# Latent roots by a Newton step, and the rotary parts of two keys between the latents' pieces

## The reference

```python
def rms_norm(x, g):
    xf = x.astype(jnp.float32)
    y = xf * lax.rsqrt(jnp.mean(xf * xf, axis=-1, keepdims=True) + EPS)
    return (y * g.astype(jnp.float32)).astype(x.dtype)
...
def apply_rope(x, cos, sin):
    half = x.shape[-1] // 2
    x1, x2 = x[..., :half], x[..., half:]
    c = cos[None, :, None, :].astype(x.dtype)
    s = sin[None, :, None, :].astype(x.dtype)
    return jnp.concatenate([x1 * c - x2 * s, x2 * c + x1 * s], axis=-1)
...
    cq, ckv, kr, dq, dkk, dvv, nq, nkv, ng = jnp.split(h @ w_in, splits, axis=-1)

    qm = (rms_norm(cq, mla_q_norm_g) @ mla_w_uq).reshape(b, t, MLA_HEADS, MLA_NOPE_DIM + MLA_ROPE_DIM)
...
    kvm = (rms_norm(ckv, mla_kv_norm_g) @ mla_w_ukv).reshape(b, t, MLA_HEADS, MLA_NOPE_DIM + MLA_V_DIM)
...
    k_rope = apply_rope(kr[:, :, None, :], *cs_mla)[:, :, 0, :]
...
    k_all = apply_rope(kv[:, :, :, 0].reshape(b, t, 3 * NSA_GROUPS, NSA_DK), *cs_nsa).reshape(b, t, 3, NSA_GROUPS, NSA_DK)
    v_all = kv[:, :, :, 1]
    k_cmp = compress_tokens(k_all[:, :, 0], cmp_pos[0], cmp_w1[0], cmp_b1[0], cmp_w2[0])
```

## Time and profile before

| | us |
|---|---|
| three timed runs | 3837.71, 3849.64, 3850.16 |
| their median | 3849.64 |
| the profiled execution | 3834.81 |
| span of the profiled execution | 3832.8 |

### The profile page before, as it was taken

How to read it: one execution, slowest core, us unless ns; L and a number is a source line. 1 busy time by engine, 2 the same in 40 slices (tenths; PEclk the granted TensorE clock), 3 DMA queues, 4 the chain that set the end, 5 groups by cost and what they waited for, 6 DMA issues and landing times. The chain is left out here.

```text
span 3832.8 us, 50696 instructions
## 1 busy us (share of the span) xinstructions
PE 3603.5 (94%) x18374; PEld 2849.2 (74%) x18374; DVE 1356.9 (35%) x1911; ACT 1271.5 (33%) x1997; POOL 1410.6 (37%) x756
## 2 busy tenths in 40 slices
PE   7999799999999999799999996999998997779998
PEld 6888566688887888566688884888886784548886
DVE  4223554552325233554552326111115203561112
ACT  4222334443224222334443224312123234234222
POOL 4444333344444444333344442323232440014443
PEclk9999899999999999899999997999998998889999
DMA  4333343223323333343223332222212322013331
GB/s 133 97 99 88 73 125 107 93 77 99 95 88 99 98 98 89 72 127 106 94 77 99 94 89 70 60 66 60 66 52 58 88 77 66 1 44 88 94 98 60
DMA packets 569026, 322.34 MB, mean 84 GB/s; under 512 B 30266, under 2 KB 563360, under 8 KB 568480
## 3 DMA queue, kind: packets, MB, share of 16 engines
q1 hardware_dynamic: 568864, 320.22, 28.7%
HBM read 318.08 MB, written 2.10 MB: 84 GB/s over the span
## 5 line engine op out<-in xcount | busy, mean ns | idle before, releaser
L857 POOL TENSOR_TENSOR w_lo<-w_raw,w_hi 128x1024 fp32r<-128x1024 f32 x516 | 1268.4, 2459 | 2154.1 <-ACT w_hi L902 2154.1
L902 ACT ACTIVATE w_hi<-w_raw 128x1024 fp32r<-128x1024 f32 x516 | 546.9, 1061 | 1846.1 <-PE psum L2086 1731.6
L2086 PE MATMUL psum<-h_hi,w_hi 128*128 128x512 f32 x1296 | 529.7, 409 | 42.8 <-DVE h_ctx_lo L1482 21.8
L2086 PE MATMUL psum<-xg_hi,w_hi 128*128 128x512 f32 x1408 | 551.7, 392 | 13.7 <-DVE xg_lo L1434 12.1
L2086 PE MATMUL psum<-xg_lo,w_hi 128*128 128x512 f32 x1408 | 549.0, 390 | 0.0
L2086 PE MATMUL psum<-xg_hi,w_lo 128*128 128x512 f32 x1408 | 548.9, 390 | 0.0
L2086 PE MATMUL psum<-h_lo,w_hi 128*128 128x512 f32 x1296 | 513.0, 396 | 0.0
L2086 PE MATMUL psum<-h_hi,w_lo 128*128 128x512 f32 x1296 | 512.9, 396 | 0.0
L2086 PE MATMUL psum<-a_hi,w_hi 128*128 128x512 f32 x1232 | 432.8, 374 | 5.0 <-DVE a_lo L1550 4.2
L2086 PE MATMUL psum<-a_hi,w_lo 128*128 128x512 f32 x1232 | 432.6, 374 | 0.0
L2086 PE MATMUL psum<-a_lo,w_hi 128*128 128x512 f32 x1232 | 432.2, 374 | 0.0
(11 more groups left out here) (420 smaller groups left out, 4350.1 us busy)
## 6 DMA issues: line engine op xcount, KB each, us to landing
w_raw<-ffn_w SPq DMA_DIRECT2D x120, 512.0 KB, 3.8
w_raw<-ffn_w_gate SPq DMA_DIRECT2D x88, 512.0 KB, 3.8
w_raw<-ffn_w_up SPq DMA_DIRECT2D x88, 512.0 KB, 3.8
ada_raw<-ada_w SPq DMA_DIRECT2D x72, 512.0 KB, 4.5
w_raw<-ffn_w_down SPq DMA_DIRECT2D x64, 512.0 KB, 4.1
w_raw<-w_in SPq DMA_DIRECT2D x60, 512.0 KB, 3.8
w_raw<-ffn_w_down SPq DMA_DIRECT2D x32, 384.0 KB, 3.4
w_raw<-w_out SPq DMA_DIRECT2D x24, 512.0 KB, 4.0
```

The source lines that it names most:

```text
L857: nc.gpsimd.tensor_tensor(w_lo[:, i, :], w_raw[:, i, :], w_hi[:, i, :].bitcast(F32), ALU.subtract).then_inc(lo_ready, 1)
L902: nc.scalar.activation(w_hi[:, pos, :], w_raw[:, pos, :], ACT.Copy).then_inc(hi_ready, 1)
L2086: last = nc.tensor.matmul(dst, w[:, pos, k * P:(k + 1) * P], rhs[g][r](k0 + k), start=k == 0 and m == 0, stop=k == nk - 1 and m == 2)
```

## The change

The diff has four parts.

- **Roots.** ScalarE now computes Abs_reciprocal_sqrt of sum / width + eps straight, and then a square of it times half the width's reciprocal, for both latents behind tile 3 (`latent_root_of`). VectorE does one Newton step on it with two scalar_tensor_tensor for each latent: (sum + width x eps) times the square, then (that - 1.5) times the root. The result has the other sign, so the latents are copied from PSUM with a scale of -1. Both reciprocals of line 1633 are gone.
- **Rotary parts of `kr` and `ck`.** On VectorE the order is now: norm of tiles 0 and 1, rotary part of `kr`, low pieces 0 and 1, norm of tile 2, rotary part of `ck`, low piece 2. ScalarE makes the high pieces 0 and 1 behind tile 4 and 2 behind tile 5.
- **Buffers.** `roped_tile` writes the cosine product in place over its input and the sine product to the third 512 columns of `normed`; `normed` is addressed flat, in pieces of 512 columns.
- **Heads.** VectorE adds `kr`'s two products once, into head 0 of `k_mla`; ScalarE copies them to heads 1 to 3 behind tile 6.

```diff
@@ -216,6 +216,7 @@
         squares = put("squares", [P, 2, TC])
         normed_at = top[0]
         normed = put("normed", [P, 2, TC])
+        normed_flat = normed[:].rearrange("p a n -> p (a n)")
         rstd_at = top[0]
         rstd = put("rstd", [P, TC])
         ident = put("ident", [P, P])
@@ -426,7 +427,8 @@
         item_done = signal("item_done", LATE_ITEMS - len(SLOT_ENDS))
         latent_sq = signal("latent_sq", 2)
         latent_sum = signal("latent_sum", 2)
-        latent_std = signal("latent_std", 2)
+        latent_std = signal("latent_std", 4)
+        latent_root = signal("latent_root", 2)
         latent_normed = signal("latent_normed", 3)
         latent_hi_ready = signal("latent_hi_ready", 3)
         latent_lo_ready = signal("latent_lo_ready", 3)
@@ -1008,6 +1010,16 @@
                 def copy(dst, src, scale=1.0):
                     return nc.scalar.activation(dst, src, ACT.Copy, scale=scale).then_inc(copied.sem, 1)
 
+                def latent_root_of(n, root, sums, width):
+                    nc.scalar.activation(root, sums, ACT.Abs_reciprocal_sqrt, bias=eps[:, 0:1], scale=1.0 / width).then_inc(latent_std.sem, 1)
+                    act.wait_ge(*latent_std(layer, 2 * n + 1))
+                    nc.scalar.activation(squares.rearrange("p a n -> p (a n)")[:, (n + 1) * T:(n + 2) * T], root, ACT.Square,
+                                         scale=(0.5 / width) ** 0.5).then_inc(latent_std.sem, 1)
+
+                def latent_high(c):
+                    act.wait_ge(*latent_normed(layer, c + 1))
+                    nc.scalar.activation(latents_hi[:, c, :], normed_flat[:, c % 2 * T:(c % 2 + 1) * T], ACT.Copy).then_inc(latent_hi_ready.sem, 1)
+
                 def used(s):
 
                     act.wait_ge(slot_used, (turn0 - 1) * SLOTS + (SLOTS + s + 1))
@@ -1056,7 +1068,7 @@
                         copy(rope_in[:, ropes % 2, :], bank, scale)
                         ropes += 1
                     else:
-                        copy(latents[:, place, :] if kind == "cq" else tok_cmp[:, 1, :], bank)
+                        copy(*((latents[:, place, :], bank, -1.0) if kind == "cq" else (tok_cmp[:, 1, :], bank)))
 
                     if s == 1:
                         act.wait_ge(*copied(layer, 2))
@@ -1069,19 +1081,21 @@
                                              ACT.Square).then_inc(latent_sq.sem, 1)
                     if s == 3:
                         act.wait_ge(*latent_sum(layer, 1))
-                        nc.scalar.activation(rstd[:, 0:T], psum[:, 2, :], ACT.Sqrt, bias=eps[:, 0:1],
-                                             scale=1.0 / MLA_QR).then_inc(latent_std.sem, 1)
+                        latent_root_of(0, rstd[:, 0:T], psum[:, 2, :], MLA_QR)
+                        act.wait_ge(*latent_sum(layer, 2))
+                        latent_root_of(1, squares[:, 0, 0:T], psum[:, 3, :], MLA_KVR)
                     if s == 4:
-                        act.wait_ge(*latent_sum(layer, 2))
-                        nc.scalar.activation(squares[:, 0, 0:T], psum[:, 3, :], ACT.Sqrt, bias=eps[:, 0:1],
-                                             scale=1.0 / MLA_KVR).then_inc(latent_std.sem, 1)
+                        for c in range(2):
+                            latent_high(c)
 
                         act.wait_ge(*lam_step(layer, 3))
                         nc.scalar.activation(lam_stats[:, 2:4], lam_stats[:, 0:2], ACT.Exp).then_inc(lam_exp.sem, 1)
+                    if s == 6:
+                        act.wait_ge(*roped(layer, 1))
+                        for h in range(1, MLA_H):
+                            nc.scalar.activation(k_mla[MLA_NOPE:MLA_QK, h, :], k_mla[MLA_NOPE:MLA_QK, 0, :], ACT.Copy)
                     if s == 5:
-                        for c in range(3):
-                            act.wait_ge(*latent_normed(layer, c + 1))
-                            nc.scalar.activation(latents_hi[:, c, :], normed[:, c % 2, 0:T], ACT.Copy).then_inc(latent_hi_ready.sem, 1)
+                        latent_high(2)
                 hidden(1)
 
                 for s in range(N_T, ROW_S0):
@@ -1572,15 +1586,13 @@
                     dve.wait_ge(*rotated(layer, ropes + 1))
                     if ropes:
                         dve.wait_ge(*roped(layer, ropes))
-                    else:
-                        dve.wait_ge(*latent_lo_ready(layer, 3))
-                    nc.vector.tensor_tensor(normed[r0:r0 + n, 0, 0:T], x, rope[r0:r0 + n, dim, :], ALU.mult)
-                    nc.vector.tensor_tensor(normed[r0:r0 + n, 1, 0:T], psum[r0:r0 + n, 2 + events % 2, :], rope[r0:r0 + n, dim + 1, :],
+                    nc.vector.tensor_tensor(x, x, rope[r0:r0 + n, dim, :], ALU.mult)
+                    nc.vector.tensor_tensor(normed_flat[r0:r0 + n, 2 * T:3 * T], psum[r0:r0 + n, 2 + events % 2, :], rope[r0:r0 + n, dim + 1, :],
                                             ALU.mult).then_inc(turn_read.sem, 1)
                     events += 1
                     dve.wait_ge(*turn_read(layer, events))
                     for dst in dsts:
-                        last = nc.vector.tensor_tensor(dst, normed[r0:r0 + n, 0, 0:T], normed[r0:r0 + n, 1, 0:T], ALU.add)
+                        last = nc.vector.tensor_tensor(dst, x, normed_flat[r0:r0 + n, 2 * T:3 * T], ALU.add)
                     last.then_inc(roped.sem, 1)
                     ropes += 1
 
@@ -1628,35 +1640,41 @@
 
 
                 root_kv = squares[:, 0, 0:T]
-                for n, root in enumerate((rstd[:, 0:T], root_kv)):
-                    dve.wait_ge(*latent_std(layer, n + 1))
-                    nc.vector.reciprocal(root, root).then_inc(turn_read.sem, 1)
+                for n, (root, width) in enumerate(((rstd[:, 0:T], MLA_QR), (root_kv, MLA_KVR))):
+                    half_square = squares.rearrange("p a n -> p (a n)")[:, (n + 1) * T:(n + 2) * T]
+                    dve.wait_ge(*latent_std(layer, 2 * n + 2))
+                    nc.vector.scalar_tensor_tensor(half_square, psum[:, 2 + n, :], width * EPS, half_square, ALU.add, ALU.mult).then_inc(turn_read.sem, 1)
                     events += 1
-                dve.wait_ge(*turn_read(layer, 2))
+                    dve.wait_ge(*turn_read(layer, n + 1))
+                    nc.vector.scalar_tensor_tensor(root, half_square, 1.5, root, ALU.subtract, ALU.mult).then_inc(latent_root.sem, 1)
+                dve.wait_ge(*latent_root(layer, 2))
 
                 def latent_low(c):
                     dve.wait_ge(*latent_hi_ready(layer, c + 1))
-                    nc.vector.tensor_tensor(latents_lo[:, c, :], normed[:, c % 2, 0:T], latents_hi[:, c, :].bitcast(F32),
+                    nc.vector.tensor_tensor(latents_lo[:, c, :], normed_flat[:, c % 2 * T:(c % 2 + 1) * T], latents_hi[:, c, :].bitcast(F32),
                                             ALU.subtract).then_inc(latent_lo_ready.sem, 1)
 
-                for c in range(3):
-                    if c == 2:
-                        latent_low(0)
-                        dve.wait_ge(*latent_lo_ready(layer, 1))
-                    nc.vector.scalar_tensor_tensor(normed[:, c % 2, 0:T], latents[:, c, :], layer_gains[:, GAIN_Q + c:GAIN_Q + c + 1],
+                def latent_norm(c):
+                    nc.vector.scalar_tensor_tensor(normed_flat[:, c % 2 * T:(c % 2 + 1) * T], latents[:, c, :], layer_gains[:, GAIN_Q + c:GAIN_Q + c + 1],
                                                    rstd[:, 0:T] if c < 2 else root_kv, ALU.mult, ALU.mult).then_inc(latent_normed.sem, 1)
+
+                latent_norm(0)
+                latent_norm(1)
+                roped_tile(rope_in[0:MLA_ROPE, 0, :], (0, MLA_ROPE, 0), [k_mla[MLA_NOPE:MLA_QK, 0, :]])
+                latent_low(0)
                 latent_low(1)
+                dve.wait_ge(*latent_lo_ready(layer, 1))
+                latent_norm(2)
+                roped_tile(rope_in[:, 1, :], (0, P, 2), [tok_cmp[:, 0, :]])
                 latent_low(2)
                 dve.wait_ge(*lam_exp(layer, 1))
                 nc.vector.scalar_tensor_tensor(lam_stats[:, 4:5], lam_stats[:, 3:4], lam_layer[:, 0:1], lam_stats[:, 2:3],
                                                ALU.subtract, ALU.subtract).then_inc(lam_step.sem, 1)
 
                 places = {"nq": lambda j: q_nsa[:, j, :], "ks": lambda j: k_slc[:], "kw": lambda j: k_win[:],
-                          "dq": lambda j: q_diff[:, j, :], "dk": lambda j: k_diff[:, j, :], "ck": lambda j: tok_cmp[:, 0, :]}
+                          "dq": lambda j: q_diff[:, j, :], "dk": lambda j: k_diff[:, j, :]}
                 for s, (kind, _, place) in enumerate(TILES):
-                    if kind == "kr":
-                        roped_tile(rope_in[0:MLA_ROPE, ropes % 2, :], (0, MLA_ROPE, 0), [k_mla[MLA_NOPE:MLA_QK, h, :] for h in range(MLA_H)])
-                    elif kind in ROPED:
+                    if kind in places:
```

## The result

| | kernel before | kernel after |
|---|---|---|
| median of seven runs, us | 3838.04 | 3807.52 |
| lowest and highest | 3834.03 to 3850.16 | 3804.75 to 3827.93 |
| the profiled execution | 3834.81 | 3804.83 |
| its span | 3832.8 | 3803.0 |
| its mean granted clock | 0.963 | 0.968 |

The ratio is 0.9924, 95% interval 0.9902 to 0.9946: the change makes the kernel 0.76% faster. The miss of the range is no larger than the scatter: 13 runs of the kernel after, in two series, have a median of 3806.3 and a mean of 3810.7.

A forecast was written before the change was run, and what follows sets the result against it. TensorE, busy nearly throughout, was taken as the bound, idle in the projections waiting for VectorE. Per layer 8.28 + 1.52 + 0.84 + 0.09 = 10.7 us, two layers 21.4: 3849.64 - 21.4 = 3828 us, range 3810 to 3840.

The forecast's parts named there:

- The root: Latents' roots in the projections: no table load, PSUM bank free 2.5 us early, the first rotation's 0.84 us wait goes.
- The order on VectorE: Projections: `tok_cmp` ready at 453.7, 1.8 us before TensorE's swap matmul wants it, so that wait (8.28 us a layer) goes.
- The key to the heads: Three adds (about 1.8 us) leave VectorE; three ScalarE copies of 0.6 us each end by 459.1, covered by 2.7 us.
- What is late next: Taps for the compression behind the swap: done at 460.8 to 462.0, TensorE asks at 462.78, so no wait.
- The clock: From swap to next regular matmul 1.57 us instead of 3.09: the cold clock's 1.52 us goes with the pause.
- The sum: Projections save 10.7 us a layer, 21.4 us in two; everything behind the swap lets the whole gain through: 3828 us.
- Slower: Rival: pauses at the attention's start double its low-clock share, 14 us lost a layer, 28 in two: 3856 us; chance 0.03.
- The two levels: Whole kernel before: median of three timed runs, 3849.64 us, taken as base, 14.8 us above the profiled execution's 3834.81.

The follow-up runs named there:

- old_roots: The kernel after with the Sqrt root and the reciprocals of before put back, the rest of the change kept: 3821.56 us, ratio 0.9949.
- roots_only: The kernel before with the new roots alone, everything else in its old order: 3844.11 us, ratio 1.0015.
- high_late: The kernel after with all three high pieces on ScalarE behind tile 5, as before: 3819.63 us, one run.
- ropes_last: The kernel after with both rotary parts behind all three low pieces, as before: 3817.84 us, one run.
- ck_late: The kernel after with the compression keys' rotary part behind the last low piece: 3817.55 us, one run.
- heads_back: The kernel after with the four adds for the heads on VectorE and no ScalarE copies: 3815.91 us, ratio 0.9943.
- before_fill8: The kernel before with 8 extra matmuls, no part of the result, behind tile 10 of the projections in each layer: 3841.27 us, ratio 1.0000.
- before_fill12: The kernel before with 12 extra matmuls, no part of the result, behind tile 10 of the projections in each layer: 3841.83 us, ratio 1.0002.

## Why the prediction was wrong

**The root: right.** ScalarE's root and square of both latents end at 440.98, VectorE's fourth operation at 442.52 (forecast 442.3), no table load ahead of them, no wait at the rotation. old_roots prices it at 1.0 us in a layer, 0.93 forecast. The load that is left near by, at 445.90, 1.28 us, for the exponential behind it, had stood in the kernel before too (445.02); nobody waits for it.

**The order on VectorE: right.** Rotary key done at 447.66 (447.2 + 0.4 for the trace's offset), `tok_cmp` at 454.01 (453.7 + 0.4), with the 1.8 us to spare that were forecast; one add of 2.18 us, caught by GpSimd. roots_only, high_late and ropes_last show that the order carries the gain, and ck_late that one of its pieces was worth 1.7 us of margin and 0.1 us of time. The catch follows what the Trainium skill states (SBUF — State Buffer, SBUF: two separate sides): a VectorE operation with two SBUF inputs and a GpSimd operation on SBUF lock each other out for the whole instruction. The trace agrees: the add takes 2.18 us instead of 0.69 and ends 0.55 us behind GpSimd's `w_lo`.

**The key to the heads: right, and not needed with the new roots.** Three copies in 1.67 us, 0.56 each (0.6 taken), done at 459.24, 3.1 us ahead of the next split. For VectorE alone I had `tok_cmp` at 455.1 to 455.5; heads_back has 455.66. The rule of the Trainium skill (ScalarE: Activation LUTs, Rules for kernel authors) to keep plain arithmetic on VectorE, which the prediction weighed, would have cost nothing here, as worked out: 154.50 and 154.53 us of projections for 154.49 and 154.44.

**What is late next: right.** The taps are done at 461.60, forecast 460.8 to 462.0.

**The clock: right.** 1.56 us from the swap to the regular pace, forecast 1.57; clock 1.00 there.

**The sum: here it failed.** For the projections it is right to 0.1 us. The step that failed is "everything behind the swap is released by it, so I let the whole gain through", and with it, in the rival Slower, "all of it shifts together". The instructions shift together; the stretches at the low clock do not. The change in time at the low clock behind the edit stood in the sum at nothing; in this pair of traces it gave 6.4 us in the attentions and 2.0 behind them. I had a change of the low-clock share in the attention only as the rival that makes it slower, through pauses at its start, and gave it 0.03 and one sign. The runs show both signs, and fill alone brings it about: the same attention took 186.7 to 189.5 us in after and its small fills, 187.2 to 190.3 in before and its fills, 193.1 in ck_late, 194.4 and 197.6 in roots_only.

**The two levels, mis-sized.** I took 3849.64, the median of three runs, as the level from which to subtract. Seven runs have 3838.04, all 84 runs of before that are on record a mean of 3841.4. That is 11.6 of the 20.5 us by the median of seven; the remaining 8.9 are, but for some tenths, the 8.4 of the low stretches. And the range ended at 3810 because I took the profiled execution with the full gain (3813.4), less a little, for a floor. Three runs that span 12.5 us, and 1909 us of unedited work behind the edit at a mean clock of 0.96, should have told me that the floor was not known: the width of the scatter belonged below the forecast as well as above.

**What the edit itself is worth.** Over the placements tried, with the fill subtracted, kernels like before have means of 3841.4, 3838.4 and 3836.2 (fill of 0, 8 and 12; average 3838.7), those like after 3810.7, 3813.5, 3816.5, 3812.7 and 3818.9 (0, 4, 8, 12 and 47; average 3814.5). The difference is 24 us; each mean carries a standard error of 0.5 to 2.6 us. The 30.5 between the two medians is this edit at this placement; 21.5 of it is measured in the projections. That the average is above 21.5 has one cause in the rows: in before_fill8 and before_fill12 the pause costs more in itself, as the projections take 165.4 to 166.7 us less the fill, not 165.2. The rest is within what so few placements can tell.

**Left open:** what decides where a low stretch begins and ends in the attention. For the two kernels traced twice it repeats there (190.23 and 190.29; 187.36 and 187.34 in layer 1 of after, though 186.68 and 187.29 in layer 0), while behind layer 1's attention it repeats for after (1907.08 and 1907.11) and not for before. The start time alone does not decide it (ck_late, roots_only), and the 12 runs of roots_only spread over 38 us, so not every kernel repeats as these two do.

## What to carry to other kernels

Ask in which order an engine's work is needed, not how much there is: moving two rotary parts up between the pieces, with the pieces' other half made earlier on the neighbour and one add for four, removed a wait of 8 us even with the old roots, while 4 us less work on the same engine in the old order left that wait as it was. When a stage behind the edit runs at less than the full clock, add its scatter to the forecast on both sides, and take the level from the mean of many runs. To learn what an edit is worth by itself, put the time that it saves back as filler matmuls, or move both kernels by a few small fills, and compare averages.

## What was not expected of the hardware

- The share of the low clock in an unedited stage changes when the stage is shifted. From 0.9 to 10.7 us of fill change one attention of 187 us by up to 3.6 us, and a kernel with 5.4 us more work was not measurably slower (1.0002 [0.9990, 1.0015]). The Trainium skill (TensorE: Matmul & The Clock Gate, What's actually happening) says of a kernel's first matmuls that the point of change varies from run to run, since the chip's own clock for it does not begin with the kernel. Behind layer 1's attention executions of before do differ (1909.06 and 1923.46 us for the same instructions), as that would allow; in the attention of layer 0 they do not (190.23 and 190.29). No run here shows the cause.
- TensorE is nearly always busy in these stretches (in the kernel after 7.59 of 8.00 us of 582 to 590, clock 0.50), and still at the low level:

```profile
582.00:590.00 8.00, 7.59 (x40) 4.03 (x40) 4.17 (x10) 2.75 (x7) 1.52 (x2) 0.50 0.42 139
```

- A copy of 32x512 on ScalarE takes 0.56 us (1.67 for three); a high piece, a copy of 128x512, takes 0.57 (1.14 for two, at 444.75 in the kernel after). Four times the partitions cost nothing here.
